# Latent attention: one score product of 96 rows in place of two of 64 and 32

## The reference, cut to what matters

```
def mla_attention(c_q, c_kv, k_r, q_norm_g, kv_norm_g, w_uq, w_ukv, cos, sin):
    q = (rms_norm(c_q, q_norm_g) @ w_uq).reshape(B, S, MLA_HEADS, MLA_NOPE + MLA_ROPE)   # 8 heads, 64 + 32
    q_nope = q[..., :MLA_NOPE]
    q_rope = apply_rope(q[..., MLA_NOPE:], cos, sin)
    kv = (rms_norm(c_kv, kv_norm_g) @ w_ukv).reshape(B, S, MLA_HEADS, MLA_NOPE + MLA_V)
    k_nope, v = kv[..., :MLA_NOPE], kv[..., MLA_NOPE:]
    k_rope = apply_rope(k_r[:, :, None, :], cos, sin)[:, :, 0, :]                        # one for all heads
    # for each block of 128 queries
    s = (einsum('bqhd,bkhd->bhqk', qn, k_nope) + einsum('bqhr,bkr->bhqk', qr, k_rope)) * scale
    p = softmax(s)
    return einsum('bhqk,bkhd->bqhd', p, v)
```

## Time and profile before

| what | value |
|---|---|
| median of 3 runs | 2761.32 us (2757.69 to 2761.82) |
| profiled execution | 2762.18 us, its span 2760.3 us |
| TensorE busy | 2580.4 us (93%) in 19296 instructions |
| VectorE busy | 1500.0 us (54%) in 2230 |
| ScalarE busy | 945.4 us (34%) in 1419 |
| GpSimd busy | 234.6 us (9%) in 218 |
| latent attention, first run | about 418 to 526 us of the span |
| latent attention, second run | about 982 to 1090 us |

### The profile page before, as it was taken

The page is one execution under the profiler, slowest core; times in us unless marked ns, Lnnn a source line. Parts: engine busy times, 40 slices in busy tenths (PEclk is TensorE's granted clock), DMA queues, the critical chain, the costliest instruction groups (busy, mean ns, idle before and its releaser), DMA issues. The chain is left out here.

```text
span 2760.3 us, 45142 instructions
## 1 busy us (share of the span) xinstructions
PE 2580.4 (93%) x19296; PEld 2077.8 (75%) x19296; DVE 1500.0 (54%) x2230; ACT 945.4 (34%) x1419; POOL 234.6 (9%) x218
## 2 busy tenths in 40 slices
PE   8999999999999998999879897899989998999998
PEld 7888776678887765788668785788878776788786
DVE  3474386633753776437356575755555496454532
ACT  4223224533222235443444332343332323433321
POOL 0000000020000000200242230100002000000011
PEclk9999998999999989999989999899999999999999
DMA  4323232122322321223200001432325111233231
GB/s 139 95 96 93 92 123 103 54 70 92 99 96 104 123 104 39 73 92 99 89 1 3 3 4 40 171 104 92 117 106 220 56 68 61 76 100 99 80 121 52
DMA packets 56108, 238.24 MB, mean 86 GB/s; under 512 B 6560, under 2 KB 7328, under 8 KB 47328
## 3 DMA queue, kind: packets, MB, share of 16 engines
q1 hardware_dynamic: 55904, 235.30, 24.5%
HBM read 231.08 MB, written 4.19 MB: 85 GB/s over the span
## 5 line engine op out<-in xcount | busy, mean ns | idle before, releaser
L347 PE MATMUL banks<-b_h,pin_pair 128*128 128x512 f32 x2304 | 528.4, 390 | 0.0
L347 PEld LDWEIGHTS banks<-b_h,pin_pair 128*128 128x128 f32 x2304 | 431.1, 188 | 89.1
L347 PE MATMUL banks<-ffh,ff_pair 128*128 128x512 f32 x2016 | 457.3, 389 | 0.0
L347 PEld LDWEIGHTS banks<-ffh,ff_pair 128*128 128x128 f32 x2016 | 378.4, 188 | 78.6
L347 PE MATMUL banks<-b_h,pab_pair 128*128 128x512 f32 x792 | 180.7, 390 | 2.3 <-DVE pab_pair L333 2.3
L347 PEld LDWEIGHTS banks<-b_h,pab_pair 128*128 128x128 f32 x792 | 148.4, 188 | 33.4 <-DVE pab_pair L333 2.7
L2832 DVE TENSOR_TENSOR ff<-ff_c,ff 128x512 fp32r<-128x512 f32 x44 | 30.5, 693 | 204.8 <-ACT ff L2820 203.4
L333 DVE TENSOR_TENSOR pin_pair<-pin_raw,pin_pair 128x1024 fp32r<-128x1024 f32 x50 | 61.3, 1226 | 134.8 <-ACT pin_pair L326 134.8
L333 DVE TENSOR_TENSOR pin_pair<-first,pin_pair 128x1024 fp32r<-128x1024 f32 x50 | 61.3, 1227 | 127.0 <-ACT pin_pair L326 127.0
L326 ACT ACTIVATE ff_pair<-ff_raw 128x1024 fp32r<-128x1024 f32 x58 | 61.5, 1060 | 182.4 <-PE banks L347 182.4
L1184 DVE SCALAR_TENSOR_TENSOR x<-banks,modf,x 128x512 f32<-128x512 f32 x32 | 24.0, 751 | 172.9 <-PE banks L365 172.9
(11 more groups left out here) (540 smaller groups left out, 4614.5 us busy)
## 6 DMA issues: line engine op xcount, KB each, us to landing
ff_raw<-in_ffn_up SPq DMA_DIRECT2D x58, 512.0 KB, 4.1
pin_raw<-in_w_in SPq DMA_DIRECT2D x50, 512.0 KB, 3.7
first<-in_w_in SPq DMA_DIRECT2D x48, 512.0 KB, 3.6
dil_ada_ring<-in_ada_w SPq DMA_DIRECT2D x24, 1024.0 KB, 7.6
dn_raw<-in_ffn_down SPq DMA_DIRECT2D x16, 1408.0 KB, 6.4
first<-in_ffn_up SPq DMA_DIRECT2D x30, 512.0 KB, 3.8
pab_raw<-in_ab_in SPq DMA_DIRECT2D x23, 512.0 KB, 3.5
dn_ada_ring<-in_ada_w SPq DMA_DIRECT2D x10, 1024.0 KB, 7.0
```

Source lines behind the costliest of these rows:

```text
L347: mm = nc.tensor.matmul(bank, w(a, k), x(b, k), start=k == 0 and i == 0, stop=k == kt - 1 and i == 2)
```

## The change

The rows of one head are placed below each other: 64 plain rows in partitions 0 to 63 and 32 rotary rows in 64 to 95, for the query (`q`, one slot a head) and for the key (`key_rows(h)`). A score is then one product of 96 rows for each head. For this

- ScalarE copies each of the four plain q tiles as two halves, both to partitions 0 to 63,
- VectorE scales each key tile as two halves, likewise,
- GpSimd copies the rotated common key to the key slots of all eight heads, and each head's rotated query to its slot: 16 copies of 32 rows,
- the keys of heads 0 to 3 lie in a tile of their own, those of heads 4 to 7 where the raw weights were,
- the `ada` ring has two slots in place of four, to make room; its loads 2 and 3 wait for folds.

```diff
-        qn, qr = sb("qn", [P, PAIRS, T]), sb("qr", [P, 2, T])
-        v, kn = (raw[:, n * TT * T:(n + 1) * TT * T].rearrange("p (j n) -> p j n", j=TT) for n in range(2))
+        q, qr = sb("q", [P, HEADS, T]), sb("qr", [P, 2, T])
+        v, later = (raw[:, n * TT * T:(n + 1) * TT * T].rearrange("p (j n) -> p j n", j=TT) for n in range(2))
+        sooner = sb("k", [P, HEADS // 2, T])
...
-        ada = Modulations(nc, m, c, sem, "mla", 16 * layer + MOD_CHUNKS, 4, m.ps[:, 7])
+        roped = sem("roped")
+        ada = Modulations(nc, m, c, sem, "mla", 16 * layer + MOD_CHUNKS, 4, m.ps[:, 7], slots=2)
...
+        def key_rows(h):
+            return sooner[:, h] if h < HEADS // 2 else later[:, h - HEADS // 2]
...
                 def score(u):
                     pair, i, s = u // TT, u % TT, 2 * (u % 2)
...
                     if i == 0:
-                        pe.wait_ge(keyed, pair + 1)
+                        pe.wait_ge(taken, 4 + 2 * pair)
+                        pe.wait_ge(keyed, 2 * pair + 2)
+                        pe.wait_ge(roped, 4 * pair + 4)
                     if u == 1:
-                        pe.wait_ge(keyed, PAIRS)
+                        pe.wait_ge(keyed, HEADS)
...
-                    at = slice(i * P, i * P + P)
                     for e in range(2):
-                        h = halves(e)
-                        nc.tensor.matmul(m.ps[:, s + e], qn[h, pair, at], kn[h, pair], start=True, stop=False)
-                    for e in range(2):
-                        r = slice(64 * e + 32 * (pair % 2), 64 * e + 32 * (pair % 2) + ROPE)
-                        mm = nc.tensor.matmul(m.ps[:, s + e], qr[r, pair // 2, at], m.kr[r], start=False, stop=True)
+                        mm = nc.tensor.matmul(m.ps[:, s + e], q[0:NOPE + ROPE, 2 * pair + e, i * P:i * P + P],
+                                              key_rows(2 * pair + e)[0:NOPE + ROPE], start=True, stop=True)
...
+            @block.gpsimd
+            def _(pool):
+                pool.wait_ge(turned, 1)
+                for h in range(0, HEADS, 2):
+                    if h == HEADS // 2:
+                        pool.wait_ge(fine, nq + nkv)
+                    for e in range(2):
+                        nc.gpsimd.tensor_copy(key_rows(h + e)[NOPE:NOPE + ROPE], m.kr[NOPE:NOPE + ROPE]).then_inc(roped, 1)
+                    pool.wait_ge(turned, 2 + h // 4)
+                    for e in range(2):
+                        at = 2 * ROPE * e + ROPE * (h // 2 % 2)
+                        nc.gpsimd.tensor_copy(q[NOPE:NOPE + ROPE, h + e], qr[at:at + ROPE, h // 4]).then_inc(roped, 1)
...
-                    nc.scalar.activation(qr[:, t] if t < 2 else qn[:, t - 2], m.ps[:, t], ACT.Copy).then_inc(taken, 1)
+                    if t < 2:
+                        nc.scalar.activation(qr[:, t], m.ps[:, t], ACT.Copy).then_inc(taken, 1)
+                        continue
+                    for e in range(2):
+                        nc.scalar.activation(q[0:NOPE, 2 * t - 4 + e], m.ps[halves(e), t], ACT.Copy).then_inc(taken, 1)
...
-                    nc.vector.tensor_tensor(kn[:, j], m.ps[:, k_bank(j)], inv[:], ALU.mult).then_inc(keyed, 1)
+                    for e in range(2):
+                        nc.vector.tensor_tensor(key_rows(2 * j + e)[0:NOPE], m.ps[halves(e), k_bank(j)], inv[halves(e)],
+                                                ALU.mult).then_inc(keyed, 1)
```

More of the change, by code:

```diff
@@ L897, in value @@
                     if i < 2:
-                        pe.wait_ge(taken, 5 + i)
+                        pe.wait_ge(taken, 8 + 2 * i)
                     for n, (k, a, b) in enumerate((k, a, b) for k in range(nkv) for a, b in ((0, 0), (0, 1), (1, 0))):
@@ L952, in _ @@
                     if j >= 2:
-                        pe.wait_ge(taken, j + 1)
+                        pe.wait_ge(taken, 2 * j)
                     if j == 3:
```

## The result

The kernel after took 2768.64 us (median of 7 runs, 2767.51 to 2771.76); seven runs of the kernel before beside them had a median of 2758.18. The ratio is 1.0039, with an interval of 1.0029 to 1.0048: slower by 10.5 us. The forecast was no change (-0.2 us, to 2761.2) with a range up to 2766.5; the time came out 10.5 us longer and above the range.

The account below looks back on a forecast made before the run. Inside the attention stage, VectorE's loop (4.18 us a unit) and TensorE's (4.17) were taken as nearly equal bounds. A run: +0.77 front, -1.19 later units, +0.3 collisions = -0.12; twice -0.2, to 2761.2 us; range 2757.0 to 2766.5.

Parts of the forecast that it names:

- The score: TensorE's 96-row score: streaming stays 1.72 us, only changes of shape saved; gain 0.39 us a unit, 0.21 kept as lower.
- reduce 11: VectorE's maximum of unit 11, counted from 0, waits 0.80 us for its score at `ada.sum`: gain 0.39.
- the distances of 4.27 and 4.28: Three distances between successive VectorE reduces, where TensorE's loop is longer, fall to 4.18: 0.29 us in all.
- The 0.30 of reduce 3: VectorE's maximum of unit 3 waits 0.30 us for its score; the prediction counted this as gained whole.
- The rival by which nothing comes back: 96-row product costs as much as both old blocks; +3.1 us, 2764.4 us; chance 0.15.
- ScalarE's halves: Stage front: eight q half copies at 0.49 us spacing delay `inv`; TensorE then stands 0.66 us before the second key product.
- The last key halves: Stage front: VectorE scales the last key tile as two halves, delaying reduce 0 by 0.61 us.
- What score 0 gives back: Stage front: the first score without shape changes on either side gains 0.50 us, 0.21 with both kept.
- GpSimd beside VectorE: GpSimd's copies near 450 us collide with VectorE's normalisation of unit 0: 0.3 us a run taken, 1.2 at worst.
- hides the entry: Reduce 2 waits 2.4 us behind TensorE's stall at 454.58, which hides the score's entry: gain only 0.21.
- this rival's 2768.5: Longer TensorE waits for L1019 in the loop bring six stretches at 1.2 GHz: +7.2 us, 2768.5; chance 0.09.
- The ring: `ada` loads 2 and 3 wait for the fold of unit 5: nothing taken, at most 0.8 us.

Follow-up runs that it names:

- two repaired kernels: Kernel after with three repairs, early first reduce and five idle products, 2758.81 us; the same with five more idle products ahead of the mix of unit 14, 2761.04 us.
- repaired version: Kernel after with three or more repairs, or kernel before with six idle products, with or without early first reduce; those near before: 2757.77 to 2759.19 us.
- the kernel with the early reduce: Kernel after with three repairs, VectorE's first reduce ahead of the last key tile, five idle products instead of seventeen: 2758.81 us, ratio 1.0003.
- the one with the short ring: Kernel before with only the ring of modulation weights cut from four slots to two: 2759.09 us, ratio 0.9998.

## Why the prediction was wrong

- **The score.** Held. Four slots of streaming in both, at most a change of shape saved, 3.8 us for TensorE's round in the plain unit (1.02 mix, 0.93 flip, the rest score), plain distances of 4.18 throughout, reduce 11 waiting 0.50 in place of 0.80. Behind reduce 3 the shorter score gives back 0.64 us a run, where 0.68 was forecast (0.39 at reduce 11, which gave 0.29, and 0.29 at the distances of 4.27 and 4.28, which gave the rest). The 0.30 of reduce 3 was not the score's but the kernel before's own stretch at 1.2 GHz (0.38). The kernel with the score in two blocks on the same rows (3.82 us) confirms that the pairs had run together, and so that row tiling had been worth as much as the 96 rows. The rival by which nothing comes back was wrong.
- **ScalarE's halves.** The mechanism was right, the size was off. "I assume that half the partitions cost the same" held for one copy (median 0.594 us). The spacing did not: 0.62 us, where 0.49 had been taken from the pair of L1019. `inv` landed 1.69 us later, 1.07 forecast.
- **The last key halves.** Also undersized: +0.82 against +0.61. What score 0 gives back was sized rightly: 0.51 us (from its start to the first product for the values 3.61 before, 3.10 after), 0.50 forecast. In all reduce 0 moved by 1.53 and not by 0.77, and by about 1.8 if the stages had begun with equal stretches at 1.2 GHz.
- **GpSimd beside VectorE.** 0.3 taken, 1.05 measured (0.72 on the normalisations, 0.33 on the shift); the bound of 1.2 held it. The six copies were placed rightly at 450 us, and one sees there four full microseconds of them back to back with VectorE's critical chain. A value near the unfavourable end would have been the one that the rows bear out. The Trainium skill, "SBUF — State Buffer", Who interferes with whom, calls the two engines' port an exclusive lock; the 0.88 that became 1.60 agrees.
- **The clock at the third score.** The step that failed. The prediction had in its rows the gap of 1.44 us and the stretch at 1.2 GHz after it, and said of reduce 2 only that the stall "hides the entry", for a gain of 0.21. It never asked what its own delays did to this gap. They add up on it: 0.77 and 0.3 as forecast, 2.57 as measured, with nothing new for TensorE to do meanwhile. The gap became 3.88, the score itself ran at 1.2 GHz, and it is what VectorE waits for: 1.8 us a run. It gave the clock a rival, but in the loop's small waits, where it came true only in two repaired kernels. That this rival's 2768.5 lies within 0.2 us of the measured 2768.64 is luck: it adds 1.2 us for each of six stretches in the loop, of which the kernel after shows none.
- **The ring.** Nothing, as forecast: shown on the kernel before, by reduces that keep their times.
- **The sum.** Forecast -0.12 a run. With the sizes measured in the first run: 1.53 for the front, 1.05 for the collisions, 1.80 for the clock, and back 0.29 at reduce 2 (its distance grew by 8.49 - 6.65 = 1.84, where the shift and the clock alone make 0.33 + 1.80), 0.38 at reduce 3 and 0.64 behind it, which is +3.07 (1.53 + 1.05 + 1.80 - 0.29 - 0.38 - 0.64). The second run has 3.20, the means of three profiles each 3.3. Twice that is 6.7 of 10.5. The kernel before, beside which the result was measured, had 2758.18 and not the 2761.32 that the forecast started from. The other 3.9 lie in code that the change doesn't touch and were in no case of the forecast; they go with the clock on the whole, and their cause is open.

No repaired version beats the kernel before: 2757.77 to 2759.19 against 2758.1 to 2759.7 for all that come near it, and no interval lies below 1. Where the repaired stage was up to 1.2 us shorter than before's (107.14 against 108.32), the times did not follow; some 0.7 of that 1.2 is the shorter stretch at 1.2 GHz at its start (5.47 us against 6.96; half of the difference, an estimate).

## What to carry to other kernels

When a change delays one engine, add the delays up on the longest gap of TensorE behind it, and look there for the granted clock: a gap that already ends at 1.2 GHz can put the very work that others wait for into that stretch. Cost a copy in a row of copies by the spacing of such a row with the same shape, not by a pair elsewhere; splitting a tile by partitions doubled its time here, on ScalarE and on VectorE. When two profiles of a stage are compared, compare what each has at 1.2 GHz at its start, too. Before giving an idle GpSimd a job, look at which VectorE instructions stand beside it, and count the longer time of each that is on the critical chain.

## What the runs showed of the hardware that was not expected

- ScalarE's copies of 64 x 512 float32 from banks take 0.594 us each and start 0.62 apart in a row; VectorE's products of that size take 1.41 a pair. Neither gains from half the partitions. GpSimd's copies of 32 x 512 take 0.611 us, as those of 128 x 512.
- A 128 x 2 operation of VectorE, 0.23 us alone, took 0.56 beside GpSimd's copies: small operations are held up too.
- TensorE's granted clock fell to 0.50 for 25 us while its records left no gap, in a kernel whose scores ran on 64 and 32 rows one at a time. And it stayed up behind a gap of 1.62 us at 484.28 in the kernel after, while it fell behind one of 1.61 and one of 1.62 in the repaired ones. In one run of a stage (the first of the kernel with the early reduce) the gap of 1.62 us at reduce 7 was followed by 2.4 GHz and that of 1.61 at reduce 13 by 1.2. A gap's length alone does not tell whether the clock falls.
- Identical code behind the changed stage was at 1.2 GHz for 133 to 136 us in profiles of the kernel before and of the one with the short ring, and for 146 to 156 in those of the kernel after.
